# Two transformer blocks on one core: output projection and gate projections between the attention's items, scores and biases in reduced passes

## The chip, the cores and the metric

One core of one Trainium2 chip runs the whole program. The metric is the device time of one execution in microseconds; the kernel before has a median of 2947.47 over 3 runs (2941.38 to 2956.33). TensorE does the matrix products (its queue is called PE here, its weight loads PEld), VectorE is DVE, ScalarE is ACT, GpSimd is POOL, and SyncE (SP) issues the loads.

## What is computed

512 tokens of width 1024 go through two layers of a first block and one layer of a second block, all in float32. Cut to what matters here:

```python
# first block, twice
xn = rms_norm(h, norm_mix[l]);  proj = xn @ w_in[l]
o_hg  = hgrn2_mixer(...)                 # linear recurrence, 4 heads of 128: channels 0..511 of mix
o_nsa = nsa_mixer(...)                   # 8 query heads, 2 key groups, dim 64: channels 512..1023
h = h + concatenate([o_hg, o_nsa]) @ w_out[l]
gu = rms_norm(h, norm_ffn[l]) @ w_ffn_in[l]
h = h + (silu(gu[..., :D_FF]) * gu[..., D_FF:]) @ w_ffn_out[l]
# second block
# "fox" attention, 8 heads of 64:  s = q @ k.T / 8 + c[t] - c[s]   (c: cumulated log forget gate)
# "diff" attention, 4 pairs of heads; then
# h += (sigmoid(xn @ w_ga) * (fox @ w_a) + sigmoid(xn @ w_gb) * (diff @ w_b)) @ w_out_2
# then cross attention to 256 memory tokens, and 32 routed experts
```

`nsa_mixer` has three branches for each query: compressed keys, selected blocks, and a window. With 512 tokens all blocks are selected, so the last two are plain causal attention.

## The kernel before

**Number format.** Most products are made as three products of float32r operands. A float32 matrix x is split in a high part (a cast to float32r) and a low part (x minus the high part), and `mm3` (L1804 to L1809) issues high times high, high times low and low times high into one PSUM bank. The weights stream through `ring` as tiles of 128x1024; POOL's `split` (L565, L568) makes `whi` (two buffers, so tile t waits until tile t-2 is used up) and `wlo`. The low and high parts of the activations are `xh` and `xl`. Other products are plain float32 (`arena`, `ekb`, `tabs` in the trace): the trace shows two records for each such matmul of PE.

**Order.** Each engine has an order of steps written out by hand (`PE_STEPS`, `ACT_STEPS`, `DVE_STEPS`, `STEPS2`), and semaphores join them. In the first block a layer is: norm, projections "feat0" to "feat19" with the recurrence's work between them, attention, "wout", norm, FFN.

**Attention.** `attend` (PE's at L2159) runs over a list of items in a software pipeline. An item k is one head (or four, for compressed keys) and one tile of 128 queries. In step s PE does the scores of item s (L2169: query times key, in the second block also `sel` times `negc` for the term c, and the causal mask as a bf16 product), the transposes of item s-3 (L2183), and the product with the values of item s-4 (L2192). DVE takes the row maximum (L1458) and copies the transposes out of PSUM (L1487), ACT takes the exponential with the row sum (L928). After the last item of a group DVE normalizes ("combine", L1418 and on, L1355 and on). Scores rotate over three PSUM banks: item k waits for the exponential of item k-3. The first block has 72 items: for each of four query tiles 8 heads of the selected branch, 2 compressed items, 8 heads of the window branch; with query tile qt an item has qt+1 blocks of 128 keys. Its queries `qr` (two heads in the two halves of the 128 rows) meet keys `kz`, in which the rows of the other group are zero. The second block has 64 items, 8 fox and 8 diff for each query tile.

**Projections at the ends.** "wout" multiplies the mix by `w_out` in eight `kouter` steps, one for each 128 rows of the weight; each goes over eight PSUM banks (24 matmuls), and its operand is split by DVE's `stream` (L1070, L1072). The first four need only the recurrence's heads. The 16 gate projections of the second block ("feat18" to "feat33") run before its attention, each evacuated by a sigmoid of ACT.

**First tiles after a norm.** `first_pair` (L1822 to L1838) works on two weight tiles at once: for each chunk c it waits for `xh` chunk c and issues four matmuls (L1829), then two for each low chunk (L1833). It waits for the splits of both tiles before it begins. The next tile's split can begin only when the pair is done.

Of the kernel before, what the change touches and what calls it, by code (L numbers as in the profile page):

```python
# [91 lines left out]
    xs=30, xsh=FFC,  # L92
# [15 lines left out]
    kz=1, dbuild=2, hid=2, kc=1, kce=1, vc=1, vcc=1,  # L108
# [13 lines left out]
    b_in=0, sel=0, trig=0, trigs=0, fl=0, fls=0, nck=0, lam=0, lams=0, fv=0, dv=0, cv=0, mrg=0, ms=0, msr=0)  # L122
# [4 lines left out]
def build(nc, ring_w, xT_in, cols_in, misc_in, tabs_in, masks_in, par_in, sel_in, pos_in, memT_in, gfin_in,  # L127
          w_gate, w_up, w_down, hm_dram, y_dram, out):
    ctx = ExitStack()
    with ctx:  # L130
# [20 lines left out]
        kz = xn[:, 0:4, :].rearrange("p (a b) t -> p a b t", b=2)  # L151
# [7 lines left out]
        misc = sb("misc", [P, MISC])  # L159
        tabs = sb("tabs", [P, 2 * T])  # L160
# [42 lines left out]
        Sst = at_(7680 + 1536, 4, P)  # L203
        act = at_(0, FFC, T)
# [35 lines left out]
        ftmp = sb("ftmp", [P, 2, T])  # L240
        ekb = sb("ekb", [P, 4, T])
# [38 lines left out]
        sel = tabs[:, :].rearrange("p (a b) -> p a b", b=P)  # L280
        negc = ekb[:, 0, :]
# [79 lines left out]
        def nsa_items():  # L361
            items = []
            for qt in range(QT):
# [35 lines left out]
        def block2_items():  # L399
            items = []  # L400
            for qt in range(QT):
                qs, n = slice(qt * P, qt * P + P), P * (qt + 1)
                this = []
                for h in range(8):
                    half = slice(64 * (h % 2), 64 * (h % 2) + 64)
                    pv = [(PS[:, 5, 64 * h:64 * h + 64], kb, fv[:, kb, 64 * h:64 * h + 64], kb == 0, kb == qt)
                          for kb in range(qt + 1)]
                    this.append(causal_item("full", qt, fq[half, h // 2, qs], fk[half, h // 2, 0:n], pv,
                                            Lt[:, qt % 2, h:h + 1], [(0, n, sel[:, h, :], negc[:, 0:n])]))
# [10 lines left out]
                def mixes(q):  # L420
                    s = slice(q * P, q * P + P)
                    return [dict(kind="mix", mixn=2 * q + 1, nb=4, src=ftmp[:, 0, :], dst=slice(0, 4), cols=s),
                            dict(kind="mix", mixn=2 * q + 2, nb=4, src=ftmp[:, 1, :], dst=slice(4, 8), cols=s,
                                 sub=True)]
# [49 lines left out]
        LAG_T, LAG_V = 3, 4  # L474

# [184 lines left out]
        def _(act_e):  # L660
# [27 lines left out]
            def late_norm(l):  # L688
# [6 lines left out]
                for c in range(KO):  # L695
                    nc.scalar.activation(sq8[:, c, :], xT[:, c, :], ACT.Square).then_inc(sems["sq"], 1)
# [41 lines left out]
            def step(l, kind, i):  # L738
# [55 lines left out]
                elif kind == "kz":  # L794
                    act_e.wait_ge(sems["rope"], nth("rope", l, 6))
                    act_e.wait_ge(sems["tile"], nth("tile", l, T_V + 2))
                    for br in range(2):
                        for g in range(2):
                            ins = nc.scalar.activation(kz[:, br, g, :], kr[:, br, :], ACT.Identity,
                                                       scale=grp[:, g:g + 1])  # L800
                    ins.then_inc(sems["kz"], 1)
# [17 lines left out]
                elif kind == "hn":  # L819
# [13 lines left out]
                    nc.scalar.activation(rrs[:, i % 2, :], lnb[:, :], ACT.Exp, scale=-0.5).then_inc(sems["hrs"], 1)  # L833
                elif kind == "attention":
# [11 lines left out]
            def step2(kind, i):  # L846
# [3 lines left out]
                elif kind == "trig":  # L850
                    act_e.wait_ge(sems["trig"], nth("trig", 0, 1))
# [48 lines left out]
                elif kind == "cross":  # L900
                    attend(l, CROSS)
# [1645 lines left out]
```

## Time and profile before

| | us |
|---|---|
| median of 3 runs | 2947.47 |
| the profiled execution | 2968.1 |
| its span, first to last instruction | 2966.3 |

| engine | busy us | share |
|---|---|---|
| PE | 2731.7 | 92% |
| POOL | 1151.4 | 39% |
| DVE | 1462.4 | 49% |
| ACT | 897.8 | 30% |

The first block's layers span about 0 to 863 and 863 to 1705, with attention from 305 to 428 and from 1148 to 1271. The second block's projections follow until 1973, its attention until 2140, the cross attention until 2323, and the experts until the end. The profiled execution took 20.6 more than the median. Times of the trace are those of this execution. A matmul record is longer than the distance to the next one, since matmuls overlap; what a matmul costs is the distance between starts.

### The profile page before, as it was taken

The page shows a single profiled execution, that of the slowest core. Times are in us where ns is not written, and L with a number is a line of the kernel's source. Part 1 is how long each engine was busy: PE and PEld are TensorE (multiplying, and loading weights), DVE is VectorE, ACT ScalarE, POOL GpSimd, SP SyncE. Part 2 cuts the span into 40 slices and gives each one's busy share as a digit, 9 for nine tenths or more (in the row PEclk, how much of TensorE's full clock was granted, in tenths as well). Part 3 has the DMA queues.
Part 4 walks back from the last instruction along what each step waited for, and adds up shares of the span by engine and source line. Part 5 has one row for each costly group of instructions (what it writes and reads, how often), then busy time and mean ns, then how long its engine had stood idle before and what let it go on. Part 6 is the DMA issues. An engine that isn't in the chain of part 4 may idle for free.

```text
span 2966.3 us, 37460 instructions
## 1 busy us (share of the span) xinstructions
PE 2731.7 (92%) x12718; PEld 2092.8 (71%) x12718; DVE 1462.4 (49%) x2107; ACT 897.8 (30%) x1468; POOL 1151.4 (39%) x768
## 2 busy tenths in 40 slices
PE   6989898999989889999999999999899699999995
PEld 4768777887867777777887777776576466666662
DVE  4673664122345854751213343015655577887785
ACT  3322322111024213311110020112202376776774
POOL 3752015666747720046666645440053011112120
PEclk9999899999999998999999999987999799999997
DMA  3213002332322111012333222320023199999995
GB/s 125 64 36 93 8 15 78 99 93 91 92 71 73 55 44 58 1 58 98 93 98 109 92 69 88 100 64 1 1 78 121 42 359 344 393 390 358 386 393 201
DMA packets 78151, 373.33 MB, mean 126 GB/s; under 512 B 11216, under 2 KB 11344, under 8 KB 53328
## 3 DMA queue, kind: packets, MB, share of 16 engines
q1 hardware_dynamic: 71888, 360.23, 34.5%
q0 software_dynamic: 5280, 8.40, 0.9%
q10 hardware_dynamic: 864, 3.15, 0.3%
q8 instruction: 71, 1.16, 0.2%
q14 instruction: 48, 0.39, 0.0%
HBM read 368.06 MB, written 12.58 MB: 128 GB/s over the span
## 4 chain that ended last, share of the span: by engine, by line
PE 83%; DVE 6%; POOL 3%; issue 3%; ACT 2%; DMA 2%; DVEq 0%; ACTq 0%; SPq 0%; POOLq 0%
PE PS L1807 16%; PE PS L1808 15%; PE PS L1809 15%; PE PS L2169 6%; PE PS L2192 4%; PE PS L2259 4%; PE PS L2260 4%; PE PS L2289 3%; PE PS L1932 2%; PE PS L1829 2%; PE PS L2183 2%; PE PS L2269 2%; PE PS L2129 2%; PE PS L1884 1%; PE PS L2247 1%
## 5 line engine op out<-in xcount | busy, mean ns | idle before, releaser
L565 POOL TENSOR_SCALAR whi<-ring 128x1024 fp32r<-128x1024 f32 x260 | 293.3, 1128 | 1210.2 <-PE PS L1809 963.5
L568 POOL TENSOR_TENSOR wlo<-ring,whi 128x1024 fp32r<-128x1024 f32 x260 | 655.6, 2522 | 21.7
L1807 PE MATMUL PS<-xh,whi 128*128 128x512 f32 x1264 | 504.9, 399 | 30.8 <-POOL wlo L568 24.3
L1808 PE MATMUL PS<-xl,whi 128*128 128x512 f32 x1264 | 496.6, 393 | 0.0
L1809 PE MATMUL PS<-xh,wlo 128*128 128x512 f32 x1264 | 496.5, 393 | 0.0
L1566 DVE TENSOR_TENSOR arena_r<-arena,arena_r 128x1024 fp32r<-128x1024 f32 x256 | 301.6, 1220 | 90.6 <-ACT arena_r L958 87.8
L1807 PEld LDWEIGHTS PS<-xh,whi 128*128 128x128 f32 x1264 | 240.3, 190 | 88.8 <-issue 17.2
L958 ACT ACTIVATE arena_r<-arena 128x1024 fp32r<-128x1024 f32 x256 | 255.9, 1050 | 91.2 <-DMA arena<-w_gate 91.0
L1808 PEld LDWEIGHTS PS<-xl,whi 128*128 128x128 f32 x1264 | 240.6, 190 | 52.2 <-issue 2.9
L1809 PEld LDWEIGHTS PS<-xh,wlo 128*128 128x128 f32 x1264 | 240.1, 190 | 50.9
L1807 PE MATMUL PS<-xs,whi 128*128 128x512 f32 x560 | 231.2, 413 | 17.4 <-DVE xs L1241 10.1
L1808 PE MATMUL PS<-xs,whi 128*128 128x512 f32 x560 | 223.8, 400 | 0.0
L1809 PE MATMUL PS<-xs,wlo 128*128 128x512 f32 x560 | 223.5, 399 | 0.0
L1458 DVE TENSOR_REDUCE nmx<-PS 128x1 f32<-128x256 f32 (+3 forms) x208 | 100.6, 484 | 239.0 <-PE PS L2169 228.9
L2259 PE MATMUL PS<-arena_r,xh 128*128 128x512 f32 x512 | 208.8, 408 | 2.0 <-DVE arena_r L1566 1.8
L2260 PE MATMUL PS<-arena_r,xh 128*128 128x512 f32 x512 | 204.1, 399 | 0.0
L2192 PE MATMUL PS<-arena,sq 128*128 128x64 f32 (+2 forms) x992 | 156.4, 290 | 12.6 <-DVE sq L1487 10.7
L631 POOL COPY idyi<-hid 64x1 int32 (+1 forms) x32 | 5.7, 178 | 407.4 <-DVE xT L1755 407.4
L2192 PEld LDWEIGHTS PS<-arena,sq 128*128 128x128 f32 x992 | 140.8, 208 | 19.7 <-DVE sq L1487 16.8
L678 ACT ACTIVATE sq<-xT 128x512 f32<-128x512 f32 x40 | 25.2, 632 | 395.3 <-DVE xT L1406 366.6
L1807 PEld LDWEIGHTS PS<-xs,whi 128*128 128x128 f32 x560 | 107.4, 192 | 47.2 <-issue 11.8
L1808 PEld LDWEIGHTS PS<-xs,whi 128*128 128x128 f32 x560 | 107.1, 191 | 28.0 <-issue 3.8
(390 smaller groups left out, 4494.0 us busy)
## 6 DMA issues: line engine op xcount, KB each, us to landing
ring<-ring_w SPq DMA_DIRECT2D x280, 512.0 KB, 3.5
arena<-w_gate SPq DMA_DIRECT2D x64, 1024.0 KB, 7.6
arena<-w_up SPq DMA_DIRECT2D x64, 1024.0 KB, 9.2
arena<-w_down SPq DMA_DIRECT2D x64, 1024.0 KB
arena<-y_dram SPq DMA_DIRECT2D x8, 512.0 KB, 7.2
xT<-xT_in SPq DMA_DIRECT2D x1, 2048.0 KB, 8.4
out<-arena SPq DMA_DIRECT2D x4, 512.0 KB, 2.6
arena<-memT_in SPq DMA_DIRECT2D x1, 1024.0 KB, 7.5
```

The costliest lines, as they stand in the source:

```text
L565: nc.gpsimd.tensor_scalar(whi[:, t % 2, :], ring[:, t % RING, :], 1.0, 0.0, ALU.mult, ALU.add).then_inc(sems["whi"], 1)
L568: nc.gpsimd.tensor_tensor(wlo[:, t % RING, :], ring[:, t % RING, :], whi[:, t % 2, :], ALU.subtract).then_inc(sems["split"], 1)
L958: nc.scalar.activation(high(w, k), loaded(w, k), ACT.Identity).then_inc(MS["high" + w], 1)
L1458: nc.vector.tensor_reduce(nmx[:, k % 4, 0:1], PS[:, k % 3, 0:it["n"]], AX.X, ALU.max, negate=True).then_inc(sems["mx"], 1)
L1566: tt(low(w, k), loaded(w, k), high(w, k), ALU.subtract).then_inc(MS["low" + w], 1)
L1807: mm(out, a[0], b[0], start=start, stop=False)
L1808: mm(out, a[0], b[1], start=False, stop=False)
L1809: return mm(out, a[1], b[0], start=False, stop=stop)
L2169: ins = mm(PS[:, k % 3, lo:hi], lhsT, rhs, start=(j == 0), stop=(j == len(it["sc"]) - 1), skip_group_check=True)
L2192: ins = mm(o, PTs[it["t"] % 2][:, b * P:b * P + P], rhs, start=start, stop=stop)
L2259: mm(PS[:, bank, :], xgT[u % 2][:, c, :], high(w, k)[:, of], start=(c == 0), stop=False)
L2260: ins = mm(PS[:, bank, :], xgT[u % 2][:, c, :], low(w, k)[:, of], start=False, stop=(c == 7))
```

## The change

In the first block:

- The recurrence's half of the output projection is cut into 32 parts of three matmuls (`out_part`), 4 for each of 8 columns of 128 outputs. The parts of columns 0 to 5 run at the end of attention steps with k from 4 to 33, four of every five steps, into PSUM bank 2; DVE adds each finished column to `xT` (`add_part`). Columns 6 and 7 run at the start of "wout", and the `kouter` steps 0 to 3 are gone. The operands `woh` and `wol` are made once by ACT and DVE, and the weight's first four tiles are laid out by columns on the host.
- Scores of the two causal branches: the float32 product of `qr` and `kz` becomes two float32r products. `qst` holds the high part of a query in the 64 rows of its group and the low part in the other 64; `kst` holds the high part of the key in both halves, or the low part in both. ACT's "qs" and "ks" and DVE's "ql" and "kl" make them; "kz" is gone.
- Scores rotate over two PSUM banks: item k waits for the exponential of item k-2.

In the second block:

- The 16 gate projections become 64 parts of six matmuls (`gate_part`) at the end of attention steps: two in each step with k below 8, one in each with k from 8 to 55. ACT copies each finished one out (`gate_evac`); the 16 sigmoids move to the merge.
- `sel` and `negc` become float32r, `negc` as a high and a low part in rows 0 to 7 and 64 to 71 of the same product. `sel` is loaded earlier and cast by ACT ("selr").
- Scores rotate over two banks here too. The mixed output of the first three query tiles is split at the end ("late chunks", items 60 to 63) instead of at each tile.

Everywhere `first_pair` is gone: the first tile after a norm is done alone, paced by the chunks, and the next one follows as an ordinary tile. In the first block's second norm ACT squares each chunk right after its `xh`.

The diff's core ("..." marks what is left out):

```diff
@@ attention items, first block
-                        sc = [(0, n, qr[:, h % 4, q], kz[:, br, g, 0:n]), (n - P, n, ident_b, causal_b)]
+                        sc = [(0, n, qst[h % 4][g][:, q], kst[br][g][0][:, 0:n]),
+                              (0, n, qst[h % 4][g][:, q], kst[br][g][1][:, 0:n]), (n - P, n, ident_b, causal_b)]
@@ second block
-                                            Lt[:, qt % 2, h:h + 1], [(0, n, sel[:, h, :], negc[:, 0:n])]))
+                                            Lt[:, qt % 2, h:h + 1], [(0, n, sel_r[:, h, :], negc_r[:, 0:n])]))
...
+        def banks(items):
+            return 3 if items is CROSS else 2
+        def out_parts(it):
+            n = (it.get("k", 0) if it else 0) - 4
+            return (n // 5, n % 5) if 0 <= n < 30 and n % 5 < 4 else None
...
+        def gate_parts(it):
+            k = it.get("k", 64) if it else 64
+            n = 2 * k if k < 8 else 8 + k
+            return range(n, n + 2 if k < 8 else n + 1) if k < 56 else range(0)
...
@@ PE
-            def first_pair(l, bank, t, high, low):
-
-                for j in range(2):
-                    pe.wait_ge(sems["split"], nth("split", l, t + j + 1))
...
+                for c in range(KO):
+                    pe.wait_ge(sems["xh"], nth("xh", l, wait + c + 1))
+                    for w in weights(t, slice(c * P, c * P + P)):
+                        mm(out, w, xh[:, c, :], start=(c == 0 and w.name == whi.name), stop=False)
+                for c in range(KO):
+                    pe.wait_ge(sems["xn"], nth("xn", l, (wait if wait_low is None else wait_low) + c + 1))
+                    ins = mm(out, whi[:, t % 2, c * P:c * P + P], xl[:, c, :], start=False, stop=(c == 7))
...
@@ PE, "wout"
-                    kouter(l, T_WO, T_WO, 0, True, False, range(4), 1)
+                    for c in (6, 7):
+                        for k in range(4):
+                            out_part(l, c, k, c - 6)
                     turn_mix(l, NSA[-1])
                     pe.wait_ge(sems["ofree"], nth("ofree", l, 12))
-                    kouter(l, T_WO, T_WO, 0, True, False, range(5, 8), 1)
+                    pe.wait_ge(sems["wadd"], nth("wadd", l, 6))
+                    kouter(l, T_WO + 4, T_WO + 4, 0, True, False, (2, 3, 5, 6, 7), 1)
                     pe.wait_ge(sems["pt"], nth("pt", l, EV["pt"]))
-                    kouter(l, T_WO, T_WO, 0, True, False, (4,), 1).then_inc(sems["tile"], 1)
-                    for k in range(1, 8):
-                        kouter(l, T_WO + k, T_WO + k, k, False, k == 7, buf=(k + 1) % 2)
+                    pe.wait_ge(sems["wadd"], nth("wadd", l, 8))
+                    kouter(l, T_WO + 4, T_WO + 4, 0, True, False, (4, 0, 1), 1).then_inc(sems["tile"], 1)
+                    for k in range(5, 8):
+                        kouter(l, T_WO + k, T_WO + k, k - 4, False, k == 7, buf=(k + 1) % 2)
@@ PE, attend
-                        if k >= 3:
-                            pe.wait_ge(sems["p"], nth("p", l, k - 2))
+                        nb = banks(items)
+                        if k >= nb:
+                            pe.wait_ge(sems["p"], nth("p", l, k - nb + 1))
...
+                    for n in gate_parts(items[s]) if items is BL2 and s < len(items) else ():
+                        gate_part(l, n)
+                    part = out_parts(items[s]) if items is NSA and s < len(items) else None
+                    if part:
+                        if part == (0, 0):
+                            pe.wait_ge(sems["wl"], nth("wl", l, 4))
+                        out_part(l, *part, 2)
```

## Rows read from the trace of the kernel before

**Rows 1.** The page: busy time by engine, and the chain that ended last.

```profile
PE 2731.7 (92%) x12718; PEld 2092.8 (71%) x12718; DVE 1462.4 (49%) x2107; ACT 897.8 (30%) x1468; POOL 1151.4 (39%) x768
...
PE 83%; DVE 6%; POOL 3%; issue 3%; ACT 2%; DMA 2%; DVEq 0%; ACTq 0%; SPq 0%; POOLq 0%
```

**Rows 2.** Windows: length, busy of PE, PEld, DVE, ACT, POOL, then TensorE clock, DMA.

```profile
305.00:323.00 18.00, 17.19 (x95) 15.48 (x95) 11.06 (x39) 6.11 (x26) 0.00 (x0) 0.65 0.01 1
323.00:353.00 30.00, 26.39 (x177) 21.92 (x178) 20.64 (x61) 11.39 (x42) 0.00 (x0) 0.94 0.01 2
...
385.00:424.00 39.00, 38.87 (x263) 29.52 (x261) 27.19 (x53) 13.04 (x34) 0.00 (x0) 1.00 0.01 2
424.00:474.00 50.00, 49.49 (x236) 40.59 (x234) 22.01 (x29) 2.84 (x4) 27.16 (x15) 1.00 0.24 74
...
1883.00:1973.00 90.00, 89.61 (x395) 73.67 (x393) 0.00 (x0) 10.97 (x19) 57.61 (x34) 1.00 0.34 105
1973.00:1986.00 13.00, 12.42 (x53) 9.61 (x53) 3.27 (x13) 5.07 (x17) 3.39 (x2) 0.64 0.13 42
1986.00:1998.00 12.00, 12.00 (x49) 9.01 (x48) 3.89 (x16) 3.62 (x16) 0.00 (x0) 0.50 0.00 0
1998.00:2046.00 48.00, 47.97 (x155) 31.53 (x155) 20.29 (x46) 9.33 (x34) 0.00 (x0) 0.51 0.00 1
2046.00:2086.00 40.00, 38.66 (x212) 24.51 (x210) 24.52 (x48) 11.40 (x35) 0.00 (x0) 1.00 0.00 1
```

**Rows 3.** Timeline of PE, first block, last query tile: start, length, what.

```profile
399.98 1.08 PE L2169 MATMUL PS<-xraw,arena 128*128 128x512 f32 x2
400.90 0.22 PE L2169 MATMUL PS<-maskb 128*128 128x128 bf16 x1
```

**Rows 4.** Timeline of PE, second block, last query tile: bias, mask, next bias.

```profile
2103.83 1.12 PE L2169 MATMUL PS<-ekb,tabs 128*128 128x512 f32 x2
2104.79 0.22 PE L2169 MATMUL PS<-maskb 128*128 128x128 bf16 x1
...
2107.28 1.12 PE L2169 MATMUL PS<-ekb,tabs 128*128 128x512 f32 x2
```

**Rows 5.** Timeline of PE, a gate projection: two starts three float32r matmuls apart.

```profile
1889.77 0.39 PE L1807 MATMUL PS<-xh,whi 128*128 128x512 f32 x1
...
1890.45 0.39 PE L1807 MATMUL PS<-xh,whi 128*128 128x512 f32 x1
```

**Rows 6.** Groups of PE by line and shape: busy, mean ns, idle before, releasers.

```profile
L1807 PE MATMUL PS<-xh,whi 128*128 128x512 f32 x1264 | 504.9, 399 | 30.8 <-POOL wlo L568 24.3 <-ACT sq L719 3.1 <-DVE xl L1480 2.1
...
L1829 PE MATMUL PS<-xh,whi 128*128 128x512 f32 x96 | 45.2, 471 | 22.5 <-ACT xh L686 14.5 <-POOL wlo L568 8.1
```

**Rows 7.** Chain that ended last, in order: start, length, what.

```profile
239.75 6.02 PE PS L1871 x48
...
474.82 2.67 POOL wlo L568
477.53 9.15 PE PS L1829 x32
486.68 3.41 PE PS L1833 x15
491.41 2.35 POOL wlo L568
```

**Rows 8.** Timeline of DVE, start of "wout": copy of the mix, then `stream`.

```profile
431.71 0.69 DVE L1482 COPY arena<-PS 128x512 f32<-128x512 f32 x1 [1.42 <-PE PS L2156]
432.52 0.43 DVE L1070 CAST xs<-arena 128x512 fp32r<-128x512 f32 x1
432.99 0.69 DVE L1072 TENSOR_TENSOR xs<-arena,xs 128x512 fp32r<-128x512 f32 x1
```

**Rows 9.** Timeline of DVE, second block: first and last operation of a combine.

```profile
2098.96 0.24 DVE L1355 RECIPROCAL Rc<-Lt 128x16 f32<-128x16 f32 x1
...
2103.11 0.69 DVE L1374 TENSOR_REDUCE small<-qgn 128x4 f32<-128x512 f32 x1
```

More of the change, by code:

```diff
@@ L203, in build @@
         Sst = at_(7680 + 1536, 4, P)
+        qst = [[arena_r[:, 1024 * j + T * g:1024 * j + T * g + T] if j < 3 else xl[:, g, :] for g in range(2)]
+               for j in range(4)]
+        woh = [arena_r[:, 9728 + T * k:9728 + T * k + T] for k in range(4)]
+        wol = [xl[:, 2 + k, :] for k in range(4)]
+        kst = [[[xh[:, 4 * br + 2 * g + part, :] for part in range(2)] for g in range(2)] for br in range(2)]
         act = at_(0, FFC, T)
@@ L897, in step2, with gate_evac @@
                     act_e.dma_start(sel, sel_in).then_inc(sems["sel"], 16)
+                elif kind == "selr":
+                    act_e.wait_ge(sems["sel"], 16)
+                    nc.scalar.activation(sel_r, sel, ACT.Identity).then_inc(sems["act_once"], 1)
                 elif kind == "attention":
                     attend(l, BL2)
+                elif kind == "merge":
+                    tables["set"] = None
+                    act_e.wait_ge(sems["evac"], nth("evac", l, 34))
+                    for c in range(8):
+                        for part in (c, 8 + c):
+                            ins = nc.scalar.activation(sga[:, part, :], sga[:, part, :], ACT.Sigmoid)
+                        ins.then_inc(sems["sgs"], 1)
                 elif kind == "cross":
                     attend(l, CROSS)
+            def gate_evac(l, n):
+                i = 18 + n // 4
+                act_e.wait_ge(sems["tile"], nth("tile", l, tile2_of(i) + 1))
+                nc.scalar.activation(sga[:, i - 18, :], PS[:, 2, :], ACT.Identity).then_inc(sems["evac"], 1)
             def attend(l, items):
@@ L1488, in attend @@
                         ins.then_inc(sems["pt"], 1)
+                    for c in late_chunks(items[s]) if items is BL2 and s < len(items) else ():
+                        v.wait_ge(sems["yh"], c + 1)
+                        nc.vector.tensor_tensor(xl[:, c, done], y_mix[c], xh[:, c, done], ALU.subtract
+                                                ).then_inc(sems["yl"], 1)
                     it = items[s - LAG_V] if 0 <= s - LAG_V < len(items) else None
@@ L2353 @@
     + [x for i in range(10, 16) for x in (("feat", i), ("rr", i - 9))] + [("tok", 1), ("rr", 7)]
-    + [("norm", 1), ("feat", 16), ("feat", 17), ("tok", 2), ("feat", 18), ("sel", 0)]
-    + [("feat", i) for i in range(19, 34)]
+    + [("norm", 1), ("sel", 0), ("feat", 16), ("feat", 17), ("tok", 2), ("selr", 0)]
     + [("attention", 0), ("merge", 0), ("kouter", 0), ("norm", 2), ("feat", 34), ("feat", 35), ("cross", 0),
```

262 lines of the change are left out of this document (172 added, 90 removed), and 8 rows, old and new, of tables (ACT_STEPS, DVE_STEPS).

## The prediction

> **What bounds the kernel now.** I read the page first: PE is busy 92% of the span and holds 83% of the chain that ended last [rows 1]. So the change is worth what it takes off PE's own path: matmul time, gaps, and stretches at the lower clock. Then the windows by stage [rows 2]. In the first block's attention the first query tile runs at a mean granted clock of 0.65 and the second at 0.94; PE has 4.4 us without work in these two (18 - 17.19 + 30 - 26.39), and the last tile none. "wout" is full. In the second block the gate projections fill 90 us at full clock; then comes the attention, and from 1977 to 2046 PE is busy without a gap but at a clock of 0.50, that is 1.2 GHz, until the wider items of the third query tile bring 2.4 GHz back. The reader is to see that a busy share of 1 hides half the speed. The groups by line [rows 6] show a third loss: of the 30.8 us that PE sat idle before `xh` by `whi` matmuls, 24.3 us ended with POOL's low part. The chain [rows 7] shows where: the pair of first tiles waits for a split (474.8), runs (477.5 to 490.1), and then PE waits for the next tile's split, which could not begin earlier (until 493.8). This stands at six places, after each norm that feeds such a projection.
>
> **Prices.** A float32 product over 512 columns costs 400.90 - 399.98 = 0.92 us of PE [rows 3]; a float32r product 0.68 / 3 = 0.226 us [rows 5]. Over 256 columns it costs 6.02 / 48 = 0.125 us [rows 7], so it scales with the columns down to there. Over 128 columns no row shows it: at best half of that, 0.06, at worst what float32 costs, 0.23; I take 0.06 because it is nearest to the 256-column row.
>
> **Term 1, scores of the first block (two layers).** 64 items per layer with 1 to 4 blocks of keys, 160 blocks in all. Each block goes from 0.23 to 2 x 0.0565 = 0.113: -18.7 us per layer at full clock (at worst -14 if 128 columns don't speed up).
>
> **Term 2, parts in the attention.** 24 parts x 3 x 0.226 = +16.3 us per layer on PE, in items 4 to 33, the first two query tiles. They fill what was idle and, being wide and dense, should bring the clock up. Half-clock time before is 18 x 0.70 + 30 x 0.12 = 16.2 us, which loses 8.1 us [rows 2]; I leave 4.5 us of loss for items 0 to 3 and the recovery: -3.6. The 4.4 us of gaps are filled: -4.4. But with shorter scores PE reaches the waits for DVE's combines sooner in the last two query tiles, where no parts run. DVE is busy 27.2 of 39 us there [rows 2], and I count 0.6 to 0.7 us for each of six combines: +4. Two score banks instead of three cost nothing in the steady state, since the next but one item starts over 3 us after the first one, and maximum and exponential take about 2. Term 1 and 2 together: -18.7 + 16.3 - 3.6 - 4.4 + 4 = -6.4, taken as **-6.5** (ends -1 and -11).
>
> The preparation (ACT's and DVE's split of queries and keys, some 7 and 11 us) lies between 240 and 300, beside the value projections and the compressed keys, whose two stretches of 14 us leave ACT and DVE waiting. I cost it at nothing; if that cover failed, at most 3 us per layer. `woh` is four ACT copies before the first exponential, and item 0 needs them no sooner than its maximum.
>
> **Term 3, "wout".** Before it is 8 steps x 24 matmuls, the 45 us behind 428 [rows 2]. After: 8 parts 5.5, the transposes 0.5, four steps 22.3. What is late next: the first remaining step needs the last mix, so its operand comes only after the copy 0.69, the cast 0.43 and the subtraction 0.69 [rows 8], with hand-overs 2 us of idle that the recurrence's rows used to cover. 30.3 against 45.3: **-15.0** per layer (-13 to -16).
>
> **Term 4, first tile of the FFN (two layers).** Before, PE idles from 473.5 to 477.5 for the second tile's split, does two tiles until 490.1, idles to 493.8, and after both idles runs some 4 us at the lower clock. After: the first tile starts at once, paced by `xh` (its last chunk is there at 480.6, the low one at 481.9), is done at about 482.5, and frees its buffer then, so the third split is over at 486. The second tile takes 5.4 us: the third starts at 487.5 to 490 instead of 493.8, and without the second slow start: **-6.5** (-2 to -9). DVE and ACT do the same work in another order; squares between the `xh` chunks fit, since DVE feeds a chunk only every 1.3 us or so.
>
> **Term 5, first tile elsewhere.** Same mechanism at the first projection of both layers and of the second block, but there is no first idle and the low parts come 5 us after the high ones, so the single tile waits longer: -3.5, -5 and -5. At the cross query projection no third tile follows and the pair was better: +1.3. Sum **-12.2** (+3 to -18).
>
> **Term 6, second block.** The gates' 64 x 6 x 0.226 = 86.8 us move into the attention and cost the same. The half-clock time before is 13 x 0.72 + 12 + 48 x 0.98 = 68.4 us; at full clock it is 34.2 us shorter. The bias goes from 0.96 us over 512 columns [rows 4] to 0.25 with the change of format: 80 blocks x 0.18 = -14.3. The step of 3.45 us [rows 4] becomes 2.75 plus a part of 1.36. Added: a combine holds DVE from 2098.96 to 2103.80 [rows 9], which the parts cover only partly, +3.5; casting `sel` before the first score, +2. POOL's 16 splits now run beside DVE's combines. -34.2 - 14.3 + 5.5 = **-43.0** (-20 to -52). The sigmoids, 16 x 0.6 us on ACT, pass under the merge, whose chunk takes PE 5.4 us.
>
> One rule stands against the clock gain. In rows 2 the clock is 0.50 with PE busy 12.00 of 12 us; the sort of work, narrow float32 products and transposes, went with it. The Trainium skill, "TensorE: Matmul & The Clock Gate", section "Why this matters for your kernels", ties the drop to idle gaps between bursts; the trace does not agree, since there is no gap. By that rule dense parts would cure nothing here and the time would be that of rival B. The skill's "SBUF — State Buffer", section "SBUF: two separate sides", says that DVE operations with two SBUF inputs and GpSimd's exclude each other; no row shown here measures it, and by it each combine could lose up to one split's 2.4 us.
>
> **Sum.** 2 x (-6.5 - 15.0 - 6.5) - 43.0 - 12.2 = -111.2. The profiled execution took 2968.1, so it would take 2856.9; against the median of 2947.5, which is 20.6 lower, the forecast is **2836 us**.
>
> **Rivals.**
> A, the single first tile gains nothing: the wait for the split is only replaced by the wait for chunks, and the sparse start lowers the clock. For it: the low chunks come late. Against: the split of the third tile clearly starts 8 us earlier. Terms 4 and 5 go: 2836 + 25 = 2861.
> B, the clock stays low in the second block's first two query tiles although parts run there. For it: narrow work still makes up half of each step. Against: in rows 2 the gates' stretch holds 1.00. Without the 34.2 us: 2870; if the 40 parts of those tiles run at half speed too, +54: 2924.
> C, the first block's attention becomes bound by the DVE and ACT hand-overs (two banks, combines, column adds), and the same with POOL's splits beside it in the second: 15 to 25 us lost, 2851 to 2861.
> D, slower: with two banks the scores wait in every item for the exponential of the item before the last. The place is the wait at the top of PE's step, 208 items. At 0.53 us per item it eats the whole 111 us; at 0.6 it gives 2961. It decides from the point where maximum plus exponential of one item take longer than one PE step and a half. Against: DVE and ACT are at 49% and 30% [rows 1], and the parts lengthen just the short steps.
>
> **How the numbers follow.** Forecast (2815 to 2850) 0.64; A 0.12; B 0.09; C 0.11; D 0.04. The ends of the terms reach 2805 below and, with A, C and the near end of B, 2880 above: range 2805 to 2880. About 0.5% (15 us) can be told from no change. Only D and the far end of B come near it: faster 0.93, within 0.03, slower 0.04.
>
> **What would show it.** Term 1: L2169 without the `xraw` float32 products of 0.92, steps of the last tile 0.47 shorter. Term 2: clock at 1.00 from item 8 or so. Term 3: "wout" of 30 us, with one gap of 2 us before its first `kouter`. Terms 4 and 5: no idle of 3.5 us to POOL after a first tile. Term 6: clock 1.00 from the first gate part on, attention with gates about 212 us. Wrong would be the forecast if the windows there show 0.5, or if PE's idle before L2169 (waiting for ACT) exceeds 10 us in all.

## The result: 35 us less, where 111 were forecast

The changed kernel takes 2913.4 us in the median of 4 runs (2903.76 to 2930.89), the kernel before 2948.4 (2941.38 to 2956.33): a ratio of 0.9875 (95% interval 0.983 to 0.9921). It is faster, as forecast, but 2836 us and the range 2805 to 2880 were wrong. The profiled execution took 2903.76 (span 2902.0).

The page of the changed kernel, the lines that answer to [rows 1]:

```profile
PE 2671.0 (92%) x12686; PEld 2046.7 (71%) x12686; DVE 1515.1 (52%) x2147; ACT 930.1 (32%) x1525; POOL 1142.4 (39%) x768
...
PE 80%; DVE 9%; issue 3%; POOL 3%; ACT 3%; DMA 1%; DVEq 0%; ACTq 0%; SPq 0%; POOLq 0%
```

PE is busy 61 us less, and DVE has 9% of the chain that ended last instead of 6%: a part of what PE won became waits for DVE. In the first attention nearly all of PE's idle time stands before the product with the values and ends with DVE's copy of the transposes: 5.2 us in the kernel before (first of these lines, windows 304.95 to 428.40), 8.4 in the changed one (302.51 to 433.12).

```profile
L2192 PE MATMUL PS<-arena,sq 128*128 128x64 f32 (+1 forms) x336 | 51.7, 284 | 5.4 <-DVE sq L1487 5.2
```

```profile
L2307 PE MATMUL PS<-arena,sq 128*128 128x64 f32 (+1 forms) x336 | 50.2, 278 | 8.6 <-DVE sq L1606 8.4
```

By stage, from windows of the changed kernel (length, busy of PE, PEld, DVE, ACT, POOL, then TensorE's granted clock, DMA): the four query tiles of the first attention, the output projection, the second block's attention, the cross attention.

```profile
303.36:334.12 30.76, 27.08 (x148) 22.73 (x147) 17.32 (x52) 7.90 (x34) 3.41 (x2) 0.81 0.06 18
334.12:363.93 29.81, 28.40 (x199) 24.03 (x198) 20.55 (x56) 9.67 (x34) 6.83 (x4) 1.00 0.12 37
363.93:393.32 29.39, 26.98 (x211) 22.52 (x210) 22.58 (x53) 11.28 (x35) 0.00 (x0) 1.00 0.01 2
393.32:433.12 39.80, 38.15 (x299) 32.34 (x298) 28.98 (x55) 12.97 (x34) 0.00 (x0) 1.00 0.00 1
433.12:468.21 35.09, 31.02 (x125) 24.76 (x125) 16.34 (x22) 4.14 (x8) 14.89 (x8) 0.90 0.19 61
1862.99:2080.54 217.55, 213.83 (x1112) 148.59 (x1112) 86.02 (x169) 53.79 (x158) 56.54 (x33) 0.99 0.13 41
2213.00:2238.51 25.51, 23.71 (x134) 16.19 (x134) 15.45 (x41) 8.83 (x32) 2.90 (x2) 1.00 0.00 1
```

Against [rows 2]: the second block is what was hoped, 0.99 where the clock was 0.50. The first query tile still stands at 0.81, the last two have 2.41 and 1.65 us without work (29.39 - 26.98 and 39.80 - 38.15) where the kernel before has 0.84 and 0.13, and the projection is at 0.90 with 4.08 us idle.

The five executions of the two kernels whose traces were taken, in us between the first and last PE instructions of a stage ("proj 2" ends at the second block's first score; "rest" is all that stands in no other column):

| kernel | att 1a | att 1b | wout a / b | FFN a / b | proj 2 | att 2 | cross | experts | rest | span |
|---|---|---|---|---|---|---|---|---|---|---|
| before | 123.4 | 123.5 | 45.1 / 45.1 | 385.4 / 384.9 | 272.0 | 166.1 | 25.4 | 649.3 | 746.1 | 2966.3 |
| before_look_1 | 123.5 | 123.5 | 45.3 / 45.1 | 385.2 / 384.9 | 272.0 | 166.1 | 25.4 | 632.5 | 742.1 | 2945.6 |
| before_look_2 | 123.6 | 123.5 | 45.1 / 45.1 | 384.7 / 384.9 | 269.4 | 160.6 | 39.2 | 643.0 | 743.0 | 2962.1 |
| after | 130.6 | 130.5 | 35.1 / 35.0 | 380.1 / 380.6 | 181.3 | 217.5 | 25.5 | 643.0 | 742.8 | 2902.0 |
| after_again | 130.5 | 130.6 | 35.0 / 35.0 | 380.0 / 380.1 | 180.5 | 217.5 | 40.8 | 633.3 | 745.2 | 2908.5 |

The table shows something that no forecast from one trace could hold. Two stages whose code the change leaves alone take one of two lengths in both kernels: the cross attention 25.5 or some 40, the experts 633 or 643 to 649. Without these two columns the kernel before takes 2291.6, 2287.7 and 2279.9, the changed one 2233.5 and 2234.4. So the change is worth 52 us in the other stages; between the medians, here and in the second set of runs below, there are 35 and 40.

### The profile page after: what moved, and what is told of

Its sections match the earlier page's. It is cut to its first block, busy times and chain, and to the rows that moved or that the text cites. A ratio compares the mean times of both kernels' runs of the same rounds, so it can differ in the third digit from the quotient of the medians.

```text
span 2902.0 us, 37535 instructions
## 1 busy us (share of the span) xinstructions
PE 2671.0 (92%) x12686; PEld 2046.7 (71%) x12686; DVE 1515.1 (52%) x2147; ACT 930.1 (32%) x1525; POOL 1142.4 (39%) x768
## 3 DMA queue, kind: packets, MB, share of 16 engines
q8 instruction: 71, 1.16, 0.2%
## 4 chain that ended last, share of the span: by engine, by line
PE 80%; DVE 9%; issue 3%; POOL 3%; ACT 3%; DMA 1%; DVEq 0%; ACTq 0%; SPq 0%; POOLq 0%
PE PS L1930 16%; PE PS L1932 16%; PE PS L1931 16%; PE PS L2284 4%; PE PS L2406 4%; PE PS L2407 4%; PE PS L2436 4%; PE PS L2307 4%; PE PS L2044 2%; PE PS L2416 2%; PE PS L2243 2%; PE PS L2298 1%; PE PS L1996 1%; PE PS L2394 1%; POOL arena L629 1%
## 5 line engine op out<-in xcount | busy, mean ns | idle before, releaser
L1931 PE MATMUL PS<-xl,whi 128*128 128x512 f32 x1376 | 540.5, 393 | 0.0
L1930 PE MATMUL PS<-xh,whi 128*128 128x512 f32 x1312 | 525.1, 400 | 14.9 <-POOL wlo L608 6.9
L1932 PE MATMUL PS<-xh,wlo 128*128 128x512 f32 x1312 | 514.0, 392 | 0.0
L1931 PEld LDWEIGHTS PS<-xl,whi 128*128 128x128 f32 x1376 | 261.3, 190 | 52.7 <-issue 2.9
L1930 PE MATMUL PS<-xs,whi 128*128 128x512 f32 x496 | 208.7, 421 | 25.6 <-DVE xs L1147 15.5
L1931 PE MATMUL PS<-xs,whi 128*128 128x512 f32 x496 | 201.1, 405 | 0.0
L1932 PE MATMUL PS<-xs,wlo 128*128 128x512 f32 x496 | 200.7, 405 | 0.0
L2307 PE MATMUL PS<-arena,sq 128*128 128x64 f32 (+2 forms) x992 | 145.6, 276 | 20.9 <-DVE sq L1606 20.0
L2307 PEld LDWEIGHTS PS<-arena,sq 128*128 128x128 f32 x992 | 128.8, 193 | 30.4 <-DVE sq L1606 29.0
L718 ACT ACTIVATE sq<-xT 128x512 f32<-128x512 f32 x40 | 25.1, 632 | 385.3 <-DVE xT L1502 357.3
L1930 PEld LDWEIGHTS PS<-xs,whi 128*128 128x128 f32 x496 | 97.0, 196 | 53.8 <-issue 11.8
L1321 DVE TENSOR_TENSOR gtmp<-PS,rrs 128x512 f32<-128x512 f32 x44 | 30.4, 691 | 199.4 <-PE PS L1932 199.4
```

Source lines behind the costliest of these rows:

```text
L1930: mm(out, a[0], b[0], start=start, stop=False)
L1931: mm(out, a[0], b[1], start=False, stop=False)
L1932: return mm(out, a[1], b[0], start=False, stop=stop)
L2307: ins = mm(o, PTs[it["t"] % 2][:, b * P:b * P + P], rhs, start=start, stop=stop)
```

## The experiments

Times in the expectations are of one layer where nothing else is said.

### The same kernels again

> The changed kernel itself, once more. The looks so far show that two stages whose code the change leaves alone take one of two lengths: the cross attention 25.5 us (granted clock 1.00) or 39 to 41 (0.50), and the experts 633 or 643. Theory (the changed kernel falls into the long cross attention in about half of its executions, and the kernel before seldom does): its times spread over 2893 to 2931 with a median near 2912, those of the kernel before over 2941 to 2960. Rival (each chip has its own speed): the times of one kernel within one job lie within 5 us.

> The kernel before, once more, to see its stages. Theory: cross attention 25.4 us at full clock as in the first look, experts 633 to 649, so that 2941 to 2968 comes from the experts and from small clock stretches. Rival (its cross attention is long as often as that of the changed kernel): 39 us.

> The kernel before, a third look with the same expectations: cross attention 25.4 us in all looks by the theory, 39 us in about half by the rival.

The changed kernel took 2910.43 (2903.89 to 2916.95, 5 runs), the kernel before, measured with it, 2950.11 (2941.01 to 2961.86, 9 runs): ratio 0.9863 (0.9834 to 0.9891). The runs of one kernel on one chip spread over 13 and 21 us, against the rival; the theory's 2893 was never seen in the changed kernel. The third trace of the kernel before has the long cross attention (39.2 us), against the theory that it has 25.4 in all of them; how often each kernel has it, three traces and two can't tell. Windows of that stage, kernel before_look_2 and kernel after_again:

```profile
2258.95:2298.19 39.24, 37.86 (x134) 26.79 (x134) 16.37 (x41) 8.81 (x32) 5.77 (x4) 0.55 0.00 0
```

```profile
2213.59:2254.39 40.80, 39.41 (x134) 27.65 (x134) 16.48 (x41) 8.82 (x32) 2.90 (x2) 0.53 0.00 1
```

The same 134 matmuls, for most of the stage at 1.2 GHz instead of 2.4. In these five traces the long experts stage has one or two waits of 4.6 to 5.1 us for the gathered `xT` (DMA) that the short one has not, and more time at half clock: 47.7 us in the changed kernel's first trace and 37.5 in after_again, which loses another 5 us. Wait and clock together make the 10 us between the two.

### DVE and POOL

> The changed kernel, with two waits added for POOL: the split of the output projection's third tile begins only after the compressed branch's combine of the first query tile, and the split of the sixth only after the first operand of the second half is made. Theory (POOL's subtraction and DVE's operations with two SBUF inputs exclude each other): the 128x8 product of that combine goes from 2.20 us back to 0.17, PE's idle of 3.20 us at 325 shrinks below 1.2 and the half-clock stretch behind it is gone (together some 4 us per layer); the subtraction in the projection goes from 2.71 to 0.69, its idle from 4.07 to about 2.1. In all the attention 126 to 127 instead of 130.4 and the projection 33 instead of 35.1 per layer. Rival (the 2.20 us is a late wait that the profile misplaces, such as one for the values' product): both operations keep their length or the idle only moves, and the attention stays within 1 us of 130.4.

```diff
+                    if t == T_WO + 2:
+                        pool.wait_ge(sems["ofree"], nth("ofree", l, 2))
+                    if t == T_WO + 5:
+                        pool.wait_ge(sems["xs"], nth("xs", l, 1))
                     (unsplit if T_CMP <= t < T_WO else split)(base, t)
```

First the changed kernel, timeline of DVE and POOL in the compressed branch's combine and at the start of "wout" (start, length, what):

```profile
323.59 0.19 DVE L1514 RECIPROCAL Rc<-Lt 128x8 f32<-128x8 f32 x1
323.64 2.36 POOL L608 TENSOR_TENSOR wlo<-ring,whi 128x1024 fp32r<-128x1024 f32 x1
323.82 2.20 DVE L1516 TENSOR_TENSOR Rc<-Rc,gates 128x8 f32<-128x8 f32 x1
326.06 0.23 DVE L1521 TENSOR_SCALAR Rc<-Rc,mats 128x8 f32<-128x8 f32 x1
...
328.47 0.32 PE L2307 MATMUL PS<-arena,sq 128*128 128x64 f32 x1 [3.20 <-DVE sq L1606]
...
440.00 0.43 DVE L1145 CAST xs<-arena 128x512 fp32r<-128x512 f32 x1
440.04 2.58 POOL L608 TENSOR_TENSOR wlo<-ring,whi 128x1024 fp32r<-128x1024 f32 x1
440.46 2.71 DVE L1147 TENSOR_TENSOR xs<-arena,xs 128x512 fp32r<-128x512 f32 x1
...
443.22 0.80 PE L1930 MATMUL PS<-xs,whi 128*128 128x512 f32 x1 [4.08 <-DVE xs L1147]
```

The multiplication of 8 elements per row takes 2.20 us and ends with POOL's subtraction. With the waits added (kernel pool_waits):

```profile
325.29 0.17 DVE L1520 TENSOR_TENSOR Rc<-Rc,gates 128x8 f32<-128x8 f32 x1
...
439.90 0.69 DVE L1151 TENSOR_TENSOR xs<-arena,xs 128x512 fp32r<-128x512 f32 x1
...
440.65 0.62 PE L1934 MATMUL PS<-xs,whi 128*128 128x512 f32 x1 [2.06 <-DVE xs L1151]
```

0.17 and 0.69 us, idle 3.20 down to 1.16 and 4.08 to 2.06: the theory. The Trainium skill's "SBUF — State Buffer", section "SBUF: two separate sides", says that a DVE operation with two SBUF inputs and a GpSimd operation that reads SBUF exclude each other. The trace agrees: 2.20 us beside POOL's subtraction, 0.17 without. The prediction named this and gave it no term in its sum. The projection takes 32.3 (33 expected), the attention 129.4 and 127.0; 126 to 127 was expected, and in the first layer the clock of the first tile took the rest (0.77 there, 0.83 in the second).

### The last mix between two columns

> The changed kernel, with the transposes of the last mix issued between the columns 6 and 7 of the output projection instead of behind both. Theory: the mix is ready at 435.0, so its copy, cast and subtraction run beside column 7 (2.8 us): PE's idle of 4.07 us falls under 0.5, the clock stays at 1.00 and the first remaining step runs at 0.226 us per matmul instead of 0.43; the projection takes 28.5 to 30 instead of 35.1 per layer. Rival (the low clock there comes from the narrow transposes, not from the idle time): the idle goes but the half-clock stretch of 5 us stays, giving 32.

```diff
                     for c in (6, 7):
                         for k in range(4):
                             out_part(l, c, k, c - 6)
-                    turn_mix(l, NSA[-1])
+                        if c == 6:
+                            turn_mix(l, NSA[-1])
```

Windows, the whole projection of kernel mix_between:

```profile
431.60:459.90 28.30, 28.30 (x125) 23.00 (x125) 16.89 (x22) 4.08 (x7) 14.74 (x8) 1.00 0.25 75
```

No idle time, clock 1.00, 28.3 instead of 35.1: 6.8 us per layer, better than the forecast's 30.3. The rival's half clock went with the idle time: the transposes are still there, but the stretch at 1.2 GHz (443.2 to 448.5 in the changed kernel) came behind 4 us without work. Behind the 2.06 us of kernel pool_waits the first matmuls run at half clock too (0.43 us each).

### Both

> The changed kernel with both edits: the last mix transposed between columns 6 and 7, and POOL's two splits kept away from DVE's operations. Theory: the projection takes 28.3 us per layer and the attention 127 to 129.4 instead of 130.5, 17 to 20 us in all against the changed kernel in the same state of the cross attention and the experts: a median of about 2895, and a ratio to the kernel before of 0.981. Rival (the gain is lost again to the clock in the next stage, as with the products of the selector): under 8 us.

2887.02 us (2872.98 to 2893.34, 5 runs), ratio 0.9793 (0.9767 to 0.9819) where the changed kernel, measured with it, has 0.9863: 23 us between the medians, 17 to 20 expected. The two stages account for 18 of them (projection 28.4 in both layers, attention 129.4 and 127.0). Its profiled execution has both short stages: a span of 2871.2.

### Parts in other items, or none

> The changed kernel, with the parts of columns 0 to 5 in the items 18 to 47 instead of 4 to 33, that is, in the second and third query tile. Theory (parts at items 4 to 7 run at half clock and so cost double, and the steps of the third tile have waits for DVE that a part fills): the first query tile falls from 30.8 to about 21 or less, the second stays near 30, the third grows from 29.4 by 12 parts of 0.68 less some 1.5 us of gaps, to about 36; the whole attention 127 to 129 instead of 130.4. Rival (the parts bring the clock up in the first tile): without them the first tile stays at half clock for most of its length, 24 us or more, and the whole is 130 or above.

> The changed kernel without parts in the first block's attention: all eight columns of the recurrence's half run in the output projection, over banks 0 to 2, with the transposes of the last mix behind the third. Scores still rotate over two banks. Theory (the parts cost their full price in the attention, because what they fill is given back elsewhere): the attention takes 130.4 - 24 x 0.68 = 114 per layer, and the projection 35.1 + 16.3 - 6.7 (idle and slow start, now covered by five columns) = 44.7; sum 159 against 165.5 of the changed kernel. Rival (the forecast's view: parts fill 4.4 us of gaps and bring the clock up, 3.6 us): the attention takes 121 or more, sum 166 or more.

> As no_parts, with the scores of the first block rotating over three banks as in the kernel before. Theory (maximum and exponential of an item take about 2 us and a step is longer than 1 us, so two banks are enough): the attention within 1.5 us of that of no_parts. Rival (two banks make the scores wait for the exponential in short steps): 4 us or more shorter per layer than no_parts. Against the kernel before (123.3 per layer) it gives the price of the scores alone: forecast -18.7, that is 104.6; half of it would be 114.

```diff
@@ parts_from_18
-            n = (it.get("k", 0) if it else 0) - 4
+            n = (it.get("k", 0) if it else 0) - 18
@@ no_parts: out_parts returns None; in "wout"
+                    for c in range(8):
+                        for k in range(4):
+                            out_part(l, c, k, c % 3)
+                        if c == 2:
+                            turn_mix(l, NSA[-1])
@@ no_parts_3banks, besides
-            return 3 if items is CROSS else 2
+            return 2 if items is BL2 else 3
```

| kernel | att a | att b | wout | first tile, clock | third tile |
|---|---|---|---|---|---|
| before | 123.4 | 123.5 | 45.1 | 21.5, 0.66 | 32.1 |
| after | 130.6 | 130.5 | 35.1 | 30.8, 0.81 | 29.4 |
| parts_from_18 | 141.0 | 137.1 | 34.3 / 35.2 | 24.7, 0.58 | 39.6 / 37.4 |
| no_parts | 125.1 | 120.4 | 47.9 / 48.0 | 25.1, 0.57 | 30.7 / 29.4 |
| no_parts_3banks | 118.7 | 120.4 | 48.1 / 49.6 | 24.6, 0.57 | 29.4 |

My theory was wrong in the first two, and in the third it held in one layer only. With parts from item 18 the attention takes 141.0 and 137.1 where 127 to 129 was expected; without parts, attention and projection together take 173.0 and 168.4 where 159 was. The 24 parts cost 5.5 to 10.1 us in the attention, not 16: in the first tile 12 parts add 6 us (24.7 to 30.8) and raise the clock from 0.58 to 0.81, in the third tile of parts_from_18 nine parts add 8 to 10. Placed later they cost more, and the second drop of the clock in parts_from_18 costs again. Moving the parts is worth 168.4 - 165.5 = 2.9 us in one layer and 173.0 - 165.7 = 7.3 in the other, and against no_parts_3banks, which shows what could be had without them, 4.4 and 1.2. Two banks cost nothing in the second layer (120.4 both), 6.4 in the first, where the clock of the second and third tile was lower. It is no wait: PE is idle for 8.5 and 9.4 us of these attentions with two banks and for 10.8 with three. Why the clock was lower was not shown.

The row that I had least expected is the last one. In the attention it is the kernel before with shorter scores, yet its first tile takes 24.6 us instead of 21.5, in both layers. The clock fell at the same place in both kernels, 0.9 us before the first score. Windows of the first tile, kernel before and kernel no_parts_3banks:

```profile
305.44:326.98 21.54, 19.76 (x111) 17.89 (x111) 12.87 (x47) 7.94 (x34) 0.00 (x0) 0.66 0.01 1
```

```profile
303.80:328.40 24.60, 21.86 (x111) 20.07 (x111) 14.20 (x49) 7.80 (x34) 0.00 (x0) 0.57 0.00 1
```

The scores' gain is 3.1 to 4.7 us in the whole attention instead of 18.7.

### The second block: parts and bias

> The changed kernel with the sixteen gate projections again ahead of the second block's attention, whose steps then have no parts; biases, banks and sigmoids as in the changed kernel. Theory (the parts hold TensorE at its high clock in the first two query tiles): the stretch from the projections' end to the merge takes 227 + 34 - (waits now filled by parts, about 4) = 255 to 262, with a clock of 0.50 for most of the first two query tiles. Rival (the clock comes from the shorter bias products and not from the parts): the clock is 0.9 or more and the stretch takes 230 or less.

> The changed kernel with the product of selector and forget-gate sum as a float32 matmul again. Theory: 80 blocks of 128 keys cost 0.18 us more each, 14.3 us in all, at full clock throughout: 241 instead of 227 for the second block's attention. Rival (the steps are bound by the DVE and ACT hand-overs, so PE's work there is partly hidden): under 8 us. Another (longer narrow float32 work lowers the clock in spite of the parts): over 25 us and a clock under 0.9 in the first two query tiles.

> As gates_first (the gate projections ahead of the second block's attention), with the product of selector and forget-gate sum as a float32 matmul again. Theory (the short float32r products between narrow ones keep the clock at 0.50 longer): the attention takes 166 to 172 us as in the kernel before, less than the 184.3 of gates_first, although each bias product is longer. Rival (the 18 us come from the two score banks or from chance): 184 + 10 = 194 or more.

```diff
@@ gates_first: gate_parts returns nothing; STEPS2
+    + [("feat", i) for i in range(18, 34)]
@@ bias_float32: the same operands read as float32
-[(0, n, sel_r[:, h, :], negc_r[:, 0:n])]
+[(0, n, sel_r[:, h, :].bitcast(F32), negc_r[:, 0:n].bitcast(F32))]
```

Projections and attention of the second block together:

| | bias float32 | bias float32r |
|---|---|---|
| gates ahead of the attention | 266.8 + 157.6 = 424.4 | 267.6 + 184.3 = 451.9 |
| gates as parts in the attention | 180.5 + 225.5 = 406.0 | 181.3 + 217.5 = 398.8 |

The kernel before has 438.1, 438.1 and 430.0. The shorter product saves 7 us beside dense parts and costs 27 without them. The 7 alone would prove little: in the eleven traces whose code of this attention is that of the changed kernel it takes 216.0 to 223.8, with none to 17 us at half clock. At equal clock it is 9.6: bias_float32 has 225.5 and parts_from_18 216.0, both at 1.00 all through. That is less than the 14.3 expected. Windows of the attention without parts, about one query tile each, kernel gates_first and kernel gates_first_bias_float32:

```profile
1948.98:1972.00 23.02, 22.88 (x95) 17.07 (x95) 7.42 (x29) 7.34 (x32) 2.90 (x2) 0.59 0.08 24
1972.00:2018.00 46.00, 45.36 (x151) 30.07 (x150) 19.25 (x43) 9.44 (x34) 0.00 (x0) 0.50 0.00 1
2018.00:2066.00 48.00, 48.00 (x197) 31.32 (x197) 22.81 (x43) 11.19 (x34) 0.00 (x0) 0.68 0.00 1
2066.00:2133.00 67.00, 66.06 (x287) 44.31 (x287) 33.09 (x54) 16.25 (x42) 0.00 (x0) 0.69 0.00 1
```

```profile
1943.82:1971.00 27.18, 27.18 (x104) 20.13 (x105) 7.44 (x29) 7.32 (x32) 2.90 (x2) 0.54 0.07 20
1971.00:2010.00 39.00, 38.97 (x157) 25.74 (x155) 18.67 (x43) 9.42 (x34) 0.00 (x0) 0.66 0.00 1
2010.00:2050.00 40.00, 38.97 (x208) 24.42 (x208) 22.24 (x43) 11.17 (x34) 0.00 (x0) 1.00 0.00 1
2050.00:2101.40 51.40, 51.07 (x294) 33.58 (x292) 32.31 (x54) 16.24 (x42) 0.00 (x0) 1.00 0.00 1
```

With the float32 product the clock is back at 1.00 in the third tile and stays; with the short one it is 0.68 and 0.69 even there. The stretch expected at 255 to 262 for gates_first takes 227.1 + 53.1 = 280: the clock was low for longer than the theory had it. gates_first_bias_float32 was expected at 166 to 172 and takes 157.6, so the direction held and the size did not. Each number is of one execution, and the attention alone moved by 5.5 us between those of the kernel before; 27 us is well above that. The whole of gates_first took 2974.90, more than the kernel before in the same set of runs (2962.94).

### The first pair again

> The changed kernel with the first two tiles after each norm done as a pair again, at all its places. Theory (the single tile is worth what the traces differ by): the FFN of each layer 5.2 us longer, the first projections 2.4, 2.0 and 2.6 longer, the cross projection 1.1 shorter: 15 to 17 us before the experts. Rival (a part of these differences came from other edits, such as the squares moved between the chunks or the state of the weight queue): under 10 us.

The edit puts `first_pair` of the kernel before back at its six places. (The prediction counts the wait for the third tile's split at all six; at the cross query no such tile follows.) FFN 384.7 and 384.7 instead of 380.1 and 380.6, second block's projections 185.8 instead of 181.3, cross query 21.0 instead of 22.0; the first layer's start lies 1.8 earlier and the second's projections 1.4 shorter, within what these two move between executions (300.1 to 306.0, and 281.8 to 287.3). Sum of the readable ones: 4.6 + 4.1 + 4.5 - 1.0 = 12.2 us, between theory and rival.

### Dense work in the cross attention, and parts in pairs

> The kernel mix_between_pool_waits with three dense float32r matmuls of 512 columns added at the end of each of the 21 steps of the cross attention, into a bank that nobody reads: work beyond the reference's. Theory (dense wide work holds the clock at 1.00 there): the stage takes 25.5 + 21 x 0.78 = 42 us or less in every execution, and the times of the kernel spread less than before (within 15 us). Rival (the clock there is decided by what ran ahead of the stage): 0.50 in some executions, with 39 + 21 x 1.5 = 70 us and a spread of over 25.

> As cross_fill_3 with one such matmul for each step. Theory: one is enough to hold the clock: the stage takes 25.5 + 21 x 0.3 = 32 us in every execution, so that the median is within 3 us of that of mix_between_pool_waits, which has 25.5 or 39. Rival: 45 us at clock 0.50 in at least some executions; median 10 us worse.

> The kernel mix_between_pool_waits with the parts in pairs: the first block's two at a time in every second or third item, the gates' two in each even item from 8 on. The matmuls are the same. Theory (each switch between float32 and float32r costs 0.1 us or more): a pair costs 1.46 instead of 1.56 in the first block and 2.93 instead of 3.14 in the second, together 12 x 0.1 x 2 + 24 x 0.2 = 7 us less. Rival (it is the column waits and the DVE that set the steps, and uneven steps bring new idle time and low clock): no gain, or up to 10 us more in the second block's attention.

```diff
@@ cross_fill_1 (3: three of them), at the end of each step
+                    for _ in range(1 if items is CROSS else 0):
+                        mm(PS[:, 6, :], xh[:, 0, 0:P], xh[:, 0, :], start=True, stop=True)
@@ double_parts
-            return (n // 5, n % 5) if 0 <= n < 30 and n % 5 < 4 else None
+            return (n // 5, n % 5) if 0 <= n < 30 and n % 5 in (0, 2) else None
-            return range(n, n + 2 if k < 8 else n + 1) if k < 56 else range(0)
+            return range(n, n + 2) if k < 8 or k % 2 == 0 and k < 56 else range(0)
```

Windows, the cross attention of kernel cross_fill_1:

```profile
2190.23:2220.45 30.22, 29.81 (x157) 19.64 (x157) 15.80 (x41) 9.05 (x32) 2.91 (x2) 1.00 0.00 1
```

30.2 us at 1.00, and 39.3 at 1.00 with three; the step after it takes 17.9 instead of 20.5 since it begins at full clock. Of the 16 profiled executions without filler, of either kernel and all variants, ten had the long stage. Two with filler don't prove "every execution"; the times speak for it in part: 2879.78 to 2890.37 and one of 2900.42 for cross_fill_1, but a spread of 21 us for cross_fill_3 where 15 was expected. cross_fill_1 is at 0.9758 (0.971 to 0.9806) of the kernel before, which the interval does not tell from the 0.9793 without filler; its median of 2884.19 was expected within 3 us of the 2887.02 of mix_between_pool_waits and is, though the two were not measured together. cross_fill_3 has 2897.74, a ratio of 0.9801. One matmul per step costs 4.7 us against the short stage and saves 9 to 11 against the long one; that this is a gain in the whole was not shown.

double_parts: a pair of gate parts takes 2.93 us instead of 2 x 1.57, a pair of the first block's 1.47 instead of 2 x 0.78, so each time PE turns to the dense matmuls and back costs 0.1 to 0.2. That the change of format is the reason is likely and not shown: the number of turns was changed, not the format. PE's idle time in the second block's attention rose from 3.71 to 7.02 us, and the stage took 221.0 instead of 217.5. The 221.0 alone lies within what this stage does by itself (216.0 to 223.8); the idle time does not, since it is 3.7 in all eleven. The ratio is 0.9775 (0.973 to 0.982), no gain, as the rival had it. The rows, kernel mix_between_pool_waits and kernel double_parts:

```profile
1842.12:2059.58 217.46, 213.75 (x1112) 148.52 (x1112) 86.03 (x169) 53.79 (x158) 56.50 (x33) 0.99 0.13 41
```

```profile
1839.85:2060.86 221.01, 213.99 (x1112) 152.98 (x1112) 82.93 (x169) 53.74 (x158) 56.35 (x33) 0.98 0.13 41
```

## Where the prediction was right and where wrong

From trace to trace, without the cross attention and the experts: forecast -111.2, measured 2233.5 - 2291.6 = -58.1, and -52 in the means of the table. Of the 53 us missed, 27 are terms 1 and 2, 10 term 3, 9 term 6 with its first tile, and 7 terms 4 and 5.

**Terms 1 and 2 failed, with the wrong sign:** +7.1 per layer against -6.5. The step that failed in its mechanism is "The 4.4 us of gaps are filled"; the prices of scores (-18.7) and parts (+16.3) and the gain in clock (-3.6) were mis-sized, all to the same side. Scores: the price of 0.113 per block was too low. Here is a part (312.03 to 312.81) and a product of one block, then a product of four blocks, in the changed kernel:

```profile
312.03 0.48 PE L1930 MATMUL PS<-arena_r,whi 128*128 128x512 f32 x1
...
312.81 0.33 PE L2284 MATMUL PS<-xh,xl 128*128 128x128 f32 x2
312.98 0.23 PE L2284 MATMUL PS<-maskb 128*128 128x128 bf16 x1
...
395.59 0.70 PE L2284 MATMUL PS<-xh,arena_r 128*128 128x512 f32 x2
396.13 0.23 PE L2284 MATMUL PS<-maskb 128*128 128x128 bf16 x1
```

Two passes over 512 columns take 396.13 - 395.59 = 0.54, not 2 x 0.226; over 128 columns 0.17. Steps of the last tile became 0.38 shorter (1.92 to 1.54), not 0.47. The busy time of PE in the last two tiles fell by 9.0 us for 112 blocks (0.08 each), so 160 blocks are worth 12.9 and not 18.7 at full clock. Parts: 0.78 instead of 0.68, 2.4 in all. Idle time: +3.1 in the last two tiles where +4 was forecast, but in the first two 4.4 became 5.1 instead of nothing; some 1.6 to 2.0 of it is POOL's split, the wait of one combine. A part stands behind the product with the values in its step, and the idle time stands before that product. Clock: before, the first tile lost 21.5 x 0.34 = 7.3 us, now 30.8 x 0.19 = 5.8, where 3.6 less was forecast. Sum 5.8 + 2.4 + 4.2 + 2.1 = 14.5, for a miss of 13.6. And the premise under term 1 fell too: the scores were priced at full clock in a tile that runs at half of it, and shorter scores alone lowered it further.

**Term 3:** 35.1 instead of 30.3. The step allowed 2 us of idle time for the hand-over of the last mix, and it was 4.08: the split of the sixth tile starts when column 7 is done and holds the subtraction (2.71 us instead of 0.69). Behind it 12 matmuls ran at half clock, 5.2 us instead of 2.7, which had no term. Both are gone in mix_between.

**Term 4:** -5.3 and -4.3 against -6.5; the first tile of the FFN has idle time of 0.91, 2.05 and 0.53 us for `xh` that I had not counted. **Term 5:** -2.4 and -1.9 where -3.5 and -5 stood, both within their own variation; the second block's tile is worth 4.5 by pair_again (-5 forecast), the cross query +1.0 (+1.3). Rival A is refuted, though the gain by pair_again is 12.2 us in all and not 25.

**Term 6:** -39.3 with its first tile, against -48. The clock came as forecast. The bias saves 8.0 to 9.6, not 14.3 (scores and bias of 512 columns: 2.02 to 1.40). Each part of six matmuls takes 1.56 in the mean instead of 1.36, a pair 2.93 instead of 2.71, about 11 us in all. Against these, PE's idle time grew by 2.0 us, less than the 5.5 added. With 1.7 us of half clock that was left, these sizes come to some 6 us more than the miss of 9; what took them back stays open. Rival B is refuted (0.99). Rival D is refuted: PE waited for the exponential for 1.0 us in all before the first block's scores, although its premise was off: in the first tile the next but one item starts after as little as 1.7 us, not over 3. Rival C was the nearest: idle time from DVE, a combine lengthened by a split; but it was priced as one lump of 15 to 25 us and given 0.11. Neither sign of being wrong came (a clock of 0.5 in the second block, 10 us of waiting for ACT); both watched other places: the wait that grew is the one for DVE's copy, 5.2 to 8.4 us per layer.

**The median.** The forecast scaled one trace. The two lengths of the cross attention and the experts stand between the 52 us of the stages and the 35 to 40 of the medians, as far as the traces show, and nothing in one trace could have said so. That the changed kernel meets the long ones more often is what its medians suggest and was not shown.

## What to carry to other kernels

Price work in a stretch that is busy at half clock by what it does to the clock: there the same shortening of a product gave 7 to 10 us beside dense parts and cost 27 without them. Bring the dense work in first, then shorten the narrow work; and put a hand-over's transposes where a column of dense work still follows. Look at every stage's length in several executions before a difference of totals is explained.

## What the runs showed of the hardware

- Float32r matmuls of 512 columns between narrow float32 ones cost 0.1 to 0.2 us more each time than their number says: three in 0.78 us, six in 1.56, twelve in 2.93, at 0.226 each 0.68, 1.36 and 2.71. The change of format is the likely reason and was not tried by itself.
- Float32r goes on getting cheaper down to 128 columns: two passes in 0.17 us, where the 256 columns of [rows 7] take 0.125 each.
- One dense matmul of 512 columns in each step was enough to see the cross attention at 2.4 GHz in its profiled execution; without it the same work ran mostly at 1.2 or all at 2.4 GHz from one execution to the next (ten and six of 16).
- A multiplication of 128x8 by DVE took 2.20 us beside POOL's subtraction and 0.17 without it; a subtraction of 128x512 took 2.71 and 0.69.
